# The operands of the expert layer shifted by 32 bytes in SBUF

## What is computed

```
def one_block(hb):                       # 128 tokens a block, d = 1024
    q = (hb @ wq).reshape(t, 8, 2, 128)
    s = einsum('thpd,hpkd->thpk', q, keys)
    ... top 16 of each half, top 16 of the 256 sums, softmax -> g, eidx
    act = gelu(einsum('thkd,td->thk', u[eidx], hb))
    return einsum('thk,thkd->td', g * act, v[eidx])
```

## Time and profile before

| | before |
|---|---|
| time, median of 3 (lowest to highest) | 2152.06 us (2151.36 to 2154.59) |
| the profiled execution: time, and span of its instructions | 2152.99 us, 2151.2 us |
| granted TensorE clock, mean over the span | 0.996 of 2.4 GHz |
| TensorE matmuls busy, share of the span | 2104.7 us, 98% |
| GpSimd busy | 1672.4 us, 78% |
| ScalarE busy | 1114.6 us, 52% |
| VectorE busy | 904.7 us, 42% |
| up pass, first matmul to last | 1366.0 to 1790.7 us |
| down pass | 1792.3 us to the end |

### The profile page before, as it was taken

How to read it: one execution, slowest core, us unless ns; L and a number is a source line. 1 busy time by engine, 2 the same in 40 slices (tenths; PEclk the granted TensorE clock), 3 DMA queues, 4 the chain that set the end, 5 groups by cost and what they waited for, 6 DMA issues and landing times.

```text
span 2151.2 us, 39494 instructions
## 1 busy us (share of the span) xinstructions
PE 2104.7 (98%) x15948; PEld 1972.7 (92%) x15948; DVE 904.7 (42%) x1919; ACT 1114.6 (52%) x1780; POOL 1672.4 (78%) x811
## 2 busy tenths in 40 slices
PE   8999999999999998999999999999999999999998
PEld 8999889999999876999978999999999998888886
DVE  5113633113112435411767315998667512212433
ACT  5555765445444346544654445455555455555555
POOL 5887667887888456788766576798676788999997
PEclk9999999999999999999999999999999999999999
DMA  7555666556555431655554355354444455555564
GB/s 298 191 185 196 255 235 255 196 195 261 191 186 196 155 138 60 213 184 194 175 179 149 138 177 206 101 189 162 139 147 144 144 175 185 200 192 195 195 196 148
DMA packets 77585, 393.70 MB, mean 183 GB/s; under 512 B 10748, under 2 KB 11900, under 8 KB 46848
## 3 DMA queue, kind: packets, MB, share of 16 engines
q1 hardware_dynamic: 77440, 391.70, 51.6%
HBM read 390.62 MB, written 1.05 MB: 182 GB/s over the span
## 4 chain that ended last, share of the span: by engine, by line
PE 74%; DVE 11%; ACT 2%; issue 1%; POOL 1%; DMA 0%; POOLq 0%; SPq 0%; DVEq 0%; ACTq 0%
PE bank L480 22%; PE bank L482 22%; PE bank L481 22%; PE bank L2698 3%; PE bank L951 3%; DVE peerR_eq L2993 1%; DVE peerR_eq L2992 1%; ACT ring_high L407 1%; DMA ring_raw<-in_stream 0%; POOL nsa_SB L1663 0%; DVE peerR_i L2994 0%; PE bank L1764 0%; DVE peerR_idx L2922 0%; DVE peerR_idx L2914 0%; DVE peerR_spare L2916 0%
## 5 line engine op out<-in xcount | busy, mean ns | idle before, releaser
L421 POOL TENSOR_TENSOR ring_low<-ring_raw,ring_high 128x2048 fp32r<-128x2048 f32 x204 | 945.0, 4645 | 341.8 <-ACT ring_high L407 341.1
L2656 POOL TENSOR_TENSOR peerS_low<-peerS_raw,peerS_high 128x512 fp32r<-128x512 f32 x510 | 679.8, 1358 | 103.6 <-ACT peerS_high L2799 102.8
L480 PE MATMUL bank<-keep_xThigh,ring_high 128*128 128x256 f32 x2112 | 592.5, 281 | 4.4 <-DVE keep_x L546 1.0
L481 PE MATMUL bank<-keep_xTlow,ring_high 128*128 128x256 f32 x2112 | 586.6, 278 | 0.0
L482 PE MATMUL bank<-keep_xThigh,ring_low 128*128 128x256 f32 x2112 | 586.5, 278 | 0.0
L407 ACT ACTIVATE ring_high<-ring_raw 128x2048 fp32r<-128x2048 f32 x207 | 396.6, 1917 | 271.8 <-PE bank L482 239.3
L2799 ACT ACTIVATE peerS_high<-peerS_raw 128x512 fp32r<-128x512 f32 x512 | 320.7, 627 | 209.4 <-PE bank L482 125.4
L480 PEld LDWEIGHTS bank<-keep_xThigh,ring_high 128*128 128x128 f32 x2112 | 398.7, 189 | 13.6 <-issue 6.8
L482 PEld LDWEIGHTS bank<-keep_xThigh,ring_low 128*128 128x128 f32 x2112 | 398.6, 189 | 0.0
L481 PEld LDWEIGHTS bank<-keep_xTlow,ring_high 128*128 128x128 f32 x2112 | 398.2, 189 | 0.3
L480 PE MATMUL bank<-keep_xThigh,peerS_high 128*128 128x256 f32 x1024 | 291.8, 285 | 3.8 <-POOL peerS_low L2656 2.8
(11 more groups left out here) (543 smaller groups left out, 3570.4 us busy)
## 6 DMA issues: line engine op xcount, KB each, us to landing
ring_raw<-in_stream SPq DMA_DIRECT2D x237, 1024.0 KB, 4.8
peerS_raw<-in_experts SPq DMA_DIRECT2D x256, 512.0 KB, 3.6
start_x<-in_x SPq DMA_DIRECT2D x2, 512.0 KB, 4.0
ring_raw<-in_stream SPq DMA_DIRECT2D x4, 256.0 KB, 5.1
context_in<-in_ctx SPq DMA_DIRECT2D x1, 1024.0 KB
mix_band_band<-in_band SPq DMA_DIRECT2D x1, 1024.0 KB, 7.5
peerT_keys_keys<-in_stream SPq DMA_DIRECT2D x1, 1024.0 KB, 5.2
out<-keep_x SPq DMA_DIRECT2D x4, 256.0 KB, 2.0
```

What stands on the lines that cost most here:

```text
L421: self.nc.gpsimd.tensor_tensor(low_, self.raw_slot(n), high.bitcast(F32), ALU.subtract).then_inc(self.low_done.sem, 1)
L480: mm(out, sh, mh, start=start, stop=False)
L481: mm(out, sh, ml, start=False, stop=False)
L2656: g_.tensor_tensor(low[:, m % 2, cut], xraw[:, m % 3, cut], high[:, m % 2, cut].bitcast(F32), ALU.subtract).then_inc(made_low.sem, 1)
```

## The change

The arena that holds the slots of the experts begins 32 bytes later, and so does the separate arena of the third gate cell. Everything that follows the first arena (`peerG2`, `peerS2`) moves with it: high, low, O1, O2, g2, raw, GT, I1T, I2T, the two gate cells and iota all go from 128 to 160 modulo 256. x, its transposed copies, A (the gelu results, at 64 modulo 256), keys, scores and everything of the other stages stay.

```
--- before.py
+++ after.py
@@ -2559,7 +2559,8 @@
         QUADS = T // 4
 
         a_at = self.keep - N * T * 4
-        side = Arena(nc, "peerS", self.base, self.base + 4 * TILE * 4)
+
+        side = Arena(nc, "peerS", self.base + 32, self.base + 32 + 4 * TILE * 4)
         high = side("high", 2 * D, dt=F32R).rearrange("p (s n) -> p s n", s=2)
         low = side("low", 2 * D, dt=F32R).rearrange("p (s n) -> p s n", s=2)
         g2 = Arena(nc, "peerG2", side.at, a_at)("g2", D)
@@ -2570,7 +2571,7 @@
         GT, I1T, I2T = (side(n, T) for n in ("GT", "I1T", "I2T"))
         GA = [side(f"GA{n}", 2 * T, dt=F32R).rearrange("p (b t) -> p b t", b=2) for n in ("high", "low")]
         iota = side("iota", P)
-        third = Arena(nc, "peerG3", self.base + 28 * 1024, a_at)
+        third = Arena(nc, "peerG3", self.base + 32 + 28 * 1024, a_at)
         third = [third(f"GA3{n}", T, dt=F32R) for n in ("high", "low")]
         cell = lambda part, n: third[part] if n == N - 1 else GA[part][:, n % 2, :]
```

## The result

| | before | after |
|---|---|---|
| median of 20 runs each | 2154.11 us (2149.45 to 2156.67) | 2156.28 us (2152.28 to 2159.77) |
| ratio, 95% interval | | 1.0014 (1.0008 to 1.0020) |
| profiled execution, its span | 2152.99, 2151.2 us | 2157.07, 2155.3 us |

The change makes the kernel about 3.0 us longer by the ratio (1.7 to 4.3 by its interval; the two medians differ by 2.2): small, but the ratio's interval lies wholly above 1. The forecast was 5.4 us less.

The account below looks back on a forecast made before the run. From 1480 us on, TensorE's matmuls by the distance between their starts were taken to bound the kernel. 2.9 + 2.5 = 5.4 us off in the up pass gave 2146.7 us against the median, range 2141 to 2158.

Parts of the forecast that it names:

- What bounds: From 1480 us on, the time is the number of TensorE's matmuls by the distance between their starts.
- I place relation 160 by the others: Up pass: 113.3 ns in every step; steps 37 to 100 lose 2.9 us, steps 101 to 127 2.5; chance 0.38.
- The first rival: Up pass: restarts choose the distance, share at 113.3 ns stays near half; 2152 give or take 2; chance 0.31.
- The second rival: Up pass: every step at 117.8 ns or worse; about 2157 us at 117.8, 2163 at 120; chance 0.22.
- The third rival: Up pass: stall gone, a distance below 113 ns (109, an estimate), 16 us off, 2136; chance 0.09.
- The terms at nothing: Steps 0 to 36, down pass, quads, and accesses of ScalarE, GpSimd, VectorE and DMA: each taken as zero.
- The rule of the Trainium skill: TensorE reads SBUF through two independent ports; by it no address could matter and the sum would be zero.

Follow-up runs that it names:

- the five kernels named above: Five follow-up kernels that keep relation 192 in the up pass; they took 112.3 to 112.9 us for steps 0 to 37.
- rest_only: Kernel before with O1, O2, raw and all gate cells 32 bytes up, high and low weights unmoved: 2161.16 us, ratio 1.0043.
- x_down: Kernel before with x and all that is kept 32 bytes down in the whole kernel, experts' slots unmoved: 2179.14 us in one run.
- both_down: x_down with the experts' slots also moved up by 224 bytes, so the up pass has relation 192 again: 2177.41 us in one run.
- o_only: Kernel before with O1 and O2 32 bytes up, raw and gate cells 256 up, iota moved, weights unmoved: 2150.43 us, ratio 0.9992.
- o_dummy: o_only plus one fp32 matmul of O1 and O2, result unused, behind the transposes of x at step 108: 2149.31 us, ratio 0.9984 to before.

## Why the prediction was wrong

- *What bounds.* Right. TensorE is full from 1480 us to the end, its matmuls' distance is the time, and the change altered nothing but that distance.
- *The step that failed* is "I place relation 160 by the others. ... The smoothest curve through the three, a + b cos + c sin, ... gives 116.65 - 2.37 - 0.81 = 113.5 ns at 160". The sum is worked out rightly; that a smooth curve holds was taken for granted. There is no smooth curve: in steps of 32 bytes the relations 0 to 224 give 120, 117, 118, 120, 120, 118, 113 or 118, and 118. Relation 160 has steps of 117.2 to 118.9 ns in the mean and no 113-step. The nearest row was there, with 117.1 ns for a product of which two thirds have relation 160, and the text set it aside as bounding little. It was within 2 ns of what came.
- *The first rival* (the mix stays) fell: no 113-step is left in any mix. Its premise held, though: restarts choose at relation 160 too, but between patterns of 117.2 and 118.7 ns, and at 128 between 118.7 and 120.
- *The second rival* is what happened, at its cheap end (117.8 ns), and for less than its price of 4.3 to 7.1 us. Behind the quads and at the end it asked 3.3 us; measured 1.8 + 0.9 = 2.7. Behind the quads the old periods of 3.72 us became 0.01 us shorter, which gives back 0.4 of the loss; in the last stretch they became 0.9 ns a matmul longer, 0.5 us in 23 steps, which the text had priced at nothing. For steps 0 to 36 it asked 3.8 less 2.8 us; measured 0.0 (up to the first quad's end). The steps did become longer, but waits for VectorE and ScalarE of 3.1 us went away. The prediction had counted the waits for GpSimd alone as cover, and those stayed (2.8 us in both). Part of this 0.0 is luck, since VectorE's weights came 4.6 us later in the execution before; the five kernels named above put it nearer 1 us, as that price did.
- *The third rival* had nothing: the shortest distance in any kernel here is 113.3.
- *The terms at nothing* were right, but for steps 0 to 37 as just said: down pass 226.7 ns, first to last matmul within 0.2 us; GpSimd's subtraction in the last stretch 1292 ns against 1293; nothing for the quads' own matmuls. rest_only shows how thin the first was: had only the gate cells moved, it would have cost 9.6 us.
- *The rule of the Trainium skill* named in the prediction (page "TensorE: Matmul & The Clock Gate", section "Step-by-step: what each phase is for", two independent read ports) does not cover this: with the same instructions the up matmuls go from 113.3 to 120 ns and the down matmuls from 226.7 to 233.3 with the operands' relation.

Shown: the relation is the cause of the lost 113-steps (x_down, both_down); which distance a restart takes at relation 192 depends on the addresses read by what ran just before (o_only against before), on whether a matmul was added there (o_dummy), and on the distance held before it (both_down against before). Not shown: why. Nothing in a trace tells which reads meet in the memory, or whether it is a matmul's own weights that count or the next ones, loaded beside it; and why relation 192 alone has 113.3 stays open. Not tried: other relations for the earlier stages, which read x against streamed weights in 2112 matmuls a line; in the trace before about a fifth of the distances between these are 117 to 119 ns.

## What to carry to other kernels

Where TensorE is full, read the distance between matmul starts and not the count of waits: in this kernel one shape at one clock differed by 6% with the address of the moving operand against that of the weights, taken modulo 256 bytes, and at one such relation by 4% with the restart. Don't interpolate between addresses; measure the eight multiples of 32, for each product by itself, and keep the best together with what runs ahead of each restart. A move that shifts two buffers together is safe only for products that read both.

## What the runs showed of the hardware

- Two distances at the same addresses are real and persistent: 113.33 or 117.78 ns at relation 192, taken at a restart and kept for up to 456 matmuls in a row (the last 19 steps, 113.33 in o_dummy, 117.78 before).
- The choice also differs between executions of code that no edit touched. The two 64-matmul groups of the mixer have 278 and 282 ns before; in the changed kernel, with the same instructions at the same addresses, they have changed places:

```profile
L480 PE MATMUL bank<-mix_rT_rT,ring_high 128*128 128x256 f32 x64 | 18.1, 283 | 0.5 <-ACT mix_grT_grT L2283 0.5
...
L480 PE MATMUL bank<-mix_mgT_mgT,ring_high 128*128 128x256 f32 x64 | 17.7, 277 | 0.3 <-PE bank L482 0.3
```

  and in rest_only both are at the short one (278 and 277). One such group turned is 192 matmuls by 4.4 ns, 0.8 us (an estimate), and so a part of what runs of one kernel differ by.
- What moves elsewhere can turn a group that nobody touched: the feed-forward's hidden tiles kept relation 192, but their group went from 277 ns (all distances 113.3) to 281 in both_down (all 117.8) and 280 in x_down (a mix of the two), though only x, which other matmuls read, had moved.
- Longer matmuls can cost nothing even with TensorE at 97% of a stretch: in the two profiled executions 3.1 us of waits in steps 0 to 37 hid 4 ns on each of some 850 matmuls.
